# A two-layer trunk of five attention branches: branch B's V product with stationary values, the opening's loads and norms in another order, and six steps of the schedule moved

## The chip, the core and the metric

The kernel runs on one core of a Trainium2 chip. Its engines are TensorE (PE: matmuls and transposes; PEld is its weight load), VectorE (DVE), ScalarE (ACT), GpSimd (POOL) and SyncE (SP, which issues nearly all DMAs). The metric is the device time of one launch in microseconds; lower is better. Tensors are float32; operands of fast matmuls are float32r pairs, a head and the rest that the head leaves.

## The reference

```python
def hybrid_layer(x, mem, ...):                  # x 512 x 1024, mem 256 x 1024
    pr = split_projection(x @ w_in)             # q, k, v of A to E, indexer, z, g
    o_a = dsa_attention(aq, ak, av, iq, ik, pr['i_w'])   # top 128 keys by indexer
    o_b = moba_attention(bq, bk, heads(pr['b_v'], N_HEADS, HEAD_DIM))
    o_c = rms_norm(diff_attention(cq, ck, cv, lam), diff_norm) * (1.0 - lam_init)
    o_d = mla_attention(qn, qr, kn, kr, dv)
    mkv = (mem @ w_mem_kv).reshape(b, mem.shape[1], 2, N_HEADS, HEAD_DIM)
    o_e = memory_attention(heads(pr['e_q'], N_HEADS, HEAD_DIM), mkv[:, :, 0], mkv[:, :, 1])
    y = o * jax.nn.silu(pr['z'].reshape(b, t, N_BRANCH, BRANCH_W))
    u = jnp.einsum('btnc,ncd->btnd', y, w_branch)
    g = jax.nn.sigmoid(pr['g'].reshape(b, t, N_BRANCH, d))
    out = jnp.sum(g * u, axis=2) @ w_out
    return layer_norm(DN_ALPHA * x + out, ln_g, ln_b)

h = layer_norm(x, ln0_g, ln0_b)                 # then hybrid_layer, twice
```

Each branch has 4 heads of 64. B is block-sparse, but with 512 tokens and blocks of 256 every earlier block is chosen, so it is plain causal attention.

## The kernel before

**Tiling.** The 512 tokens are 4 tiles of 128; D = 1024 is 8 slabs of 128. A product of float32 accuracy is three passes (`product3`, L811 to L813): head by head, rest by head, head by rest. Weights come by DMA into raw slots; ACT rounds their head, POOL subtracts for the rest (L795): a `split` step.

**The list.** `plan()` writes one list of steps that every engine walks in order, doing its own share of each. Its backbone is `grp` steps, PE's products: chunk c, unit u (two slabs of a projection chunk, or 128 output columns of a gate chunk), part t. The chunks follow ORDER: IX (the indexer), E, A1, A0, B1, B0, gE0, gE1, gB0, gB1, C0, C1, gA0, gA1, D0, D1, DU, gC0, gC1, gD0, gD1, O0, O1. A gate chunk's unit has four parts for the gate and a fifth (t = 4) for the branch product; behind the fifth DVE multiplies the two (L1712). Attention steps are spread between two groups named in PLACES. Since an engine never passes an entry of its own list, a step that waits holds back everything behind it on that engine.

**Attention steps.** `qt` transposes queries and keys on PE (L993, L1002), `ev` and `er` copy head and rest out (ACT, then DVE; for D L1534 and L1536), `S` is the scores (L1036) with mask and maximum on DVE (L1591) and exponential on ACT, `T` transposes probabilities (L1049), `V` multiplies by the values. A unit i is head i // 4, tile i % 4; tile t has t + 1 key blocks. Branches in WIDE take `wide_steps`: V has the values' head and rest side by side as the stationary operand and moves the probabilities, also as head and rest (L1066, 4 or 8 matmuls a pair of tiles, up to 256 columns). For that DVE also computes the rest of the probabilities (`pr`, L1464) and of the values (`vr`, L1456), adds up the halves (`fa`, L1471, L1477) and multiplies later (`fin`, L1489). The other branches take the narrow V: probabilities stationary, 64 columns of values moving in plain float32 (L1083: 2, 4, 6 and 8 matmuls for the tiles of a head, 20 in all). The indexer's top 128 of each row are found by sixteen rounds of MAX8 and MATCH_REPLACE8 on DVE (`top`, `take`).

**Branch C** has two maps, hence two scores a unit; its `fin` (L1615 to L1619) takes the norm's squares. **DU** expands D's latents; its part t lies in two PSUM banks which ACT empties (L1107, `mla_keys` among them), and two pairs of banks alternate.

**The opening of layer 0.** SP loads mem, x tile 0, quarter 0 of the memory weights (mk0), the norm's gains, x1, its bias, mk1, x2, mk2, mk3, then weights, x3 among them. `mkv` multiplies the memory by mk0 to mk3 in two halves (L908, L911); `ln0` normalizes tile t (sums, root, scale, ACT's L1116, gain L1374; the bias is POOL's for tiles 0 and 1, DVE's L1379 for 2 and 3); `xj` transposes a tile (L930), ACT and DVE make it the stationary head and rest (L1445). ACT's queue writes the transposed memory to DRAM (1 MB) for layer 1. The first product of IX follows `mv`, ACT's copy of the memory values.

**The end.** Behind O1's parts DVE adds the residual (L1719) and normalizes (`l1`, `l2`), tile by tile.

## Time and profile before

| | us |
|---|---|
| three timed runs, median (lowest to highest) | 1339.69 (1339.42 to 1339.84) |
| the profiled execution, its own time | 1343.1 |
| its span in the trace | 1341.5 |
| PE busy | 1307.1 |
| DVE, POOL, ACT busy | 707.8, 663.4, 662.8 |
| mean granted clock | 0.995 |

How to read it: PE is busy in nearly the whole span, so an idle or longer stretch of PE is what time can be won from or lost to; the other engines matter where PE waits for them. Matmuls overlap in the trace, so a group's own time is from its start to the next group's start, some 0.16 us less than its span. Rows in brackets `[0.65 <-DVE ...]` give the idle time before and what ended it.

### The profile page before, as it was taken

How to read it: one execution, taken by the hardware profiler on the slowest of the kernel's cores; microseconds unless marked ns; L12 is line 12 of the kernel's file. 1: busy time of each engine (PE TensorE's matmuls, PEld its weight loads, DVE VectorE, ACT ScalarE, POOL GpSimd, SP SyncE). 2: the span in 40 equal slices, each digit the busy share in tenths (PEclk: the TensorE clock that was granted, in tenths of full speed). 3: DMA queues.
4: the chain of work that ended last, by engine and by line, in shares of the span. 5: the costliest groups of instructions: out<-in, count | busy, mean ns of one | idle time of the engine just before them, and what ended most of it. 6: DMA issues, size and time to landing. Idle time of an engine off the chain costs nothing.

```text
span 1341.5 us, 18893 instructions
## 1 busy us (share of the span) xinstructions
PE 1307.1 (97%) x6744; PEld 1108.3 (83%) x6744; DVE 707.8 (53%) x1700; ACT 662.8 (49%) x1326; POOL 663.4 (49%) x838
## 2 busy tenths in 40 slices
PE   6999999999999999999999999999999999999996
PEld 5888888888888998888887888888888889888885
DVE  4746686554347464513355577675534664454135
ACT  3555445365477475523235552554646665654232
POOL 3443453354565454467435335434445553645774
PEclk8999999999999999999999999999999999999998
DMA  7322232132332143242413223322223213323321
GB/s 278 105 79 64 83 98 79 50 94 64 87 98 59 45 120 109 59 112 77 137 42 109 79 64 92 97 60 73 83 63 103 71 52 88 101 60 92 92 91 63
DMA packets 147053, 116.47 MB, mean 87 GB/s; under 512 B 5520, under 2 KB 131856, under 8 KB 146704
## 3 DMA queue, kind: packets, MB, share of 16 engines
q1 hardware_dynamic: 146816, 114.22, 28.9%
q8 instruction: 54, 0.88, 0.3%
q10 hardware_dynamic: 144, 1.05, 0.2%
q14 instruction: 39, 0.32, 0.1%
HBM read 112.10 MB, written 3.15 MB: 86 GB/s over the span
## 4 chain that ended last, share of the span: by engine, by line
PE 80%; DVE 12%; ACT 4%; issue 2%; DMA 1%; SPq 0%; DVEq 0%; ACTq 0%
PE product L811 19%; PE product L813 18%; PE product L812 18%; PE scores L1036 3%; PE context L1083 3%; PE transposed L1049 3%; PE branch_product L811 3%; PE branch_product L812 3%; PE branch_product L813 3%; PE context L1066 2%; ACT score_operands L1107 1%; DVE index_scores L1568 1%; PE product L911 1%; DVE top_eight L1574 1%; DMA merged<-in_w_mem_kv_dram 1%
## 5 line engine op out<-in xcount | busy, mean ns | idle before, releaser
L795 POOL TENSOR_TENSOR weights_rest<-raw_weights,weights_head 128x320 fp32r<-128x320 f32 (+3 forms) x672 | 542.5, 838 | 391.4 <-ACT weights_head L1107 391.2
L811 PE MATMUL product<-weights_head,stationary_head 128*128 128x512 f32 (+3 forms) x768 | 290.7, 379 | 3.0 <-issue 2.1
L813 PE MATMUL product<-weights_head,stationary_rest 128*128 128x512 f32 (+3 forms) x768 | 284.6, 371 | 0.0
L812 PE MATMUL product<-weights_rest,stationary_head 128*128 128x512 f32 (+3 forms) x768 | 284.5, 370 | 0.0
L1107 ACT ACTIVATE weights_head<-raw_weights 128x1280 fp32r<-128x1280 f32 (+4 forms) x178 | 197.7, 1113 | 142.1 <-PE product L813 116.5
L811 PE MATMUL product<-stationary_head,weights_head 128*128 128x512 f32 x640 | 260.4, 407 | 0.0
L813 PE MATMUL product<-stationary_head,weights_rest 128*128 128x512 f32 x640 | 250.4, 391 | 0.0
L812 PE MATMUL product<-stationary_rest,weights_head 128*128 128x512 f32 x640 | 250.3, 391 | 0.0
L780 POOL TENSOR_TENSOR merged<-merged,activated 128x256 f32<-128x256 f32 x128 | 94.0, 756 | 242.5 <-DVE activated L1712 242.5
L811 PEld LDWEIGHTS product<-weights_head,stationary_head 128*128 128x128 f32 x768 | 144.7, 188 | 25.5 <-issue 3.0
L813 PEld LDWEIGHTS product<-weights_head,stationary_rest 128*128 128x128 f32 x768 | 144.5, 188 | 23.8
L812 PEld LDWEIGHTS product<-weights_rest,stationary_head 128*128 128x128 f32 x768 | 144.9, 189 | 19.8
L1241 ACT ACTIVATE probabilities<-probabilities,negated_maxima 128x256 f32<-128x256 f32 (+3 forms) x160 | 86.3, 539 | 136.3 <-DVE negated_maxima L1591 134.1
L813 PEld LDWEIGHTS product<-stationary_head,weights_rest 128*128 128x128 f32 x640 | 120.1, 188 | 26.9
L811 PEld LDWEIGHTS product<-stationary_head,weights_head 128*128 128x128 f32 x640 | 120.5, 188 | 20.3
L812 PEld LDWEIGHTS product<-stationary_rest,weights_head 128*128 128x128 f32 x640 | 120.8, 189 | 19.3
L1712 DVE SCALAR_TENSOR_TENSOR activated<-activated,branch_product 128x512 f32<-128x512 f32 x64 | 43.9, 686 | 131.6 <-PE branch_product L813 128.8
L1306 ACT ACTIVATE activated<-product 128x512 f32<-128x512 f32 x80 | 47.8, 597 | 124.3 <-PE product L813 124.1
L1591 DVE CUSTOM_DVE_ANT_0 probabilities<-scores,consts_sb 128x256 f32<-128x256 f32 (+3 forms) x136 | 60.4, 444 | 62.9 <-PE scores L1036 62.0
L1036 PE MATMUL scores<-score_operands 128*128 128x256 f32 (+7 forms) x288 | 77.3, 323 | 2.5 <-DVE negated_maxima L1591 2.4
L1036 PEld LDWEIGHTS scores<-score_operands 96*128 96x128 f32 (+1 forms) x288 | 52.1, 189 | 15.0 <-DVE negated_maxima L1591 6.8
L811 PE MATMUL branch_product<-branch_out_T_head,weights_head 128*128 128x512 f32 x160 | 64.1, 400 | 0.0
(232 smaller groups left out, 1879.1 us busy)
## 6 DMA issues: line engine op xcount, KB each, us to landing
raw_weights<-in_w_in_dram SPq DMA_DIRECT2D x104, 512.0 KB, 3.7
raw_weights<-in_w_in_dram SPq DMA_DIRECT2D x72, 256.0 KB, 2.9
raw_weights<-in_w_branch_dram SPq DMA_DIRECT2D x80, 128.0 KB, 3.7
raw_weights<-in_w_out_dram SPq DMA_DIRECT2D x16, 512.0 KB, 3.7
merged<-in_w_mem_kv_dram SPq DMA_DIRECT2D x8, 512.0 KB, 7.2
raw_weights<-in_w_in_dram SPq DMA_DIRECT2D x8, 416.0 KB, 3.1
raw_weights<-in_w_in_dram SPq DMA_DIRECT2D x8, 296.0 KB, 4.6
residual<-in_x_dram SPq DMA_DIRECT2D x4, 512.0 KB, 11.5
```

The lines of the kernel that those rows point to most:

```text
L780: ins = nc.gpsimd.tensor_tensor(m[:, part], m[:, part], TH[:, s, part], ALU.add)
L795: ins = nc.gpsimd.tensor_tensor(WL[:, sw, part], RAW[:, sr, part], WH[:, sw, part].bitcast(F32), ALU.subtract)
L811: nc.tensor.matmul(dst, sh, mh, start=start, stop=False)
L812: nc.tensor.matmul(dst, sh, ml, start=False, stop=False)
L813: return nc.tensor.matmul(dst, sl, mh, start=False, stop=stop)
L1036: last = nc.tensor.matmul(S[:, 0:w], lhs, rhs, start=i == 0, stop=i == len(passes) - 1)
L1049: last = nc.tensor.transpose(TP[:, i * P:(i + 1) * P], src[:, i * P:(i + 1) * P], ident)
L1107: return nc.scalar.activation(dst, src, ACT.Copy, scale=scale)
L1241: nc.scalar.activation(p, p, ACT.Exp, bias=NMX[:, m:m + 1], scale=-1.0, accum_out=RS[:, j % 2, 2 * t + u % 2 if b == "C" else t:(2 * t + u ...
L1306: nc.scalar.activation(TH[:, s, :], G[u % 2][:], ACT.Tanh, scale=0.5).then_inc(act_out.sem, act_out.step((c, u)))
L1591: nc.vector.tensor_tensor_reduce(probs(b, u)[:, 0:w], S[:, 0:w], bias, -SCALE[b], -TAKEN, ALU.add, ALU.min, NMX[:, u % 4:u % 4 + 1]).then_ ...
L1712: nc.vector.scalar_tensor_tensor(out=TH[:, s, :], in0=TH[:, s, :], scalar=1.0, in1=U[:], op0=ALU.add, op1=ALU.mult).then_inc(used.sem, not ...
```

## The change

Seven things, all in the list of steps or in what they touch:

1. **Opening.** mk1 is loaded directly behind mk0, then gains, bias (with a semaphore of its own), x1; mk2, mk3 come behind the first raw weights, x2 and x3 behind the second. The memory's write to DRAM is issued at `ek`. `mkv` waits for each piece of memory and weights as it comes to it. `ln0` is split into sums, scale and gain, and the start of the list is written in another order.
2. **IX.** Group (2, 2) stands ahead of (0, 3), and tile 3's `xj` stands between the two (in both layers); `ek` comes behind (0, 3). The index transposes begin at (E, 0, 3).
3. **B** is in WIDE. Its attention begins at (gE0, 1, 0) instead of (gE0, 0, 4); the rounds for tile 3 run from (gE0, 3, 0) to (gB0, 0, 1) instead of (gE0, 2, 0) to (gE1, 3, 4).
4. **C**: `fin` of heads 0 to 2 comes one step later in the list.
5. **DU**: part 2 uses the banks G2 and G3.
6. **D** attention begins at (gC0, 0, 3) instead of (gC0, 0, 2).
7. **The end**: `l2` of tile 1 comes behind group (O1, 3, 2) instead of (O1, 2, 2).

```diff
-WIDE = "AD"
+WIDE = "ABD"
@@ diff_steps
-                second.append(("fin", "C", (i - 3) // NT))
+        if i >= 7 and i % NT == 3 or i == UNITS + 2:
+            second.append(("fin", "C", (i - 4) // NT if i % NT == 3 else NH - 1))
@@ PLACES
-    ("index transposes", ("E", 0, 2), ("E", 2, 1), 0.0),
+    ("index transposes", ("E", 0, 3), ("E", 2, 1), 0.0),
-    ("B attention", ("gE0", 0, 4), ("gE1", 3, 3), 0.0),
-    ("top of tile 3", ("gE0", 2, 0), ("gE1", 3, 4), 0.0),
+    ("B attention", ("gE0", 1, 0), ("gE1", 3, 3), 0.0),
+    ("top of tile 3", ("gE0", 3, 0), ("gB0", 0, 1), 0.0),
-    ("D attention", ("gC0", 0, 2), ("gC1", 3, 3), 0.0),
+    ("D attention", ("gC0", 0, 3), ("gC1", 3, 3), 0.0),
@@ plan
-    start = [("ln0", 0), ("ln0", 1), ("ez",), ("mkv", 0), ("ln0", 2), ("xj", 0, 0), ("xj", 0, 1), splits[0], splits[1], ("ln0", 3),
-             ("mkv", 1), ("xj", 1, 0), ("xj", 1, 1), ("mv",), splits[2], ("ln0", 4)]
+    start = [("ln0", 0, part) for part in ("sums", "scale", "gain")]
+    start += [("ln0", 1, "sums"), splits[0], ("ln0", 1, "scale"), ("ln0", 1, "gain"), ("mkv", 0), ("xj", 0, 0), ("xj", 0, 1), ("ez",),
+              splits[1], ("ln0", 2, "sums"), ("ln0", 2, "scale"), ("ln0", 3, "sums"), ("ln0", 2, "gain"), ("mkv", 1), ("mv",),
+              ("xj", 1, 0), ("xj", 1, 1), ("ln0", 3, "scale"), splits[2]]
-    extra[at[(ORDER[0], 1, 1)]] += [("xj", 2, 0), ("xj", 2, 1)]
-    extra[at[(ORDER[0], 2, 1)]] += [("xj", 3, 0), ("xj", 3, 1)]
-    extra[at[(ORDER[0], 2, 2)]].append(("ek",))
+    extra[at[(ORDER[0], 1, 1)]] += [("xj", 2, 0), ("xj", 2, 1), ("ln0", 3, "gain")]
+    extra[at[(ORDER[0], 2, 2)]] += [("xj", 3, 0), ("xj", 3, 1)]
+    extra[at[(ORDER[0], 0, 3)]].append(("ek",))
-    extra[at[("O1", 2, 2)]].append(("l2", 1))
+    extra[at[("O1", 3, 2)]].append(("l2", 1))
@@ DU's banks
+            return {1: (("U", U), ("TP", TP)), 2: (("G2", G[2]), ("G3", G[3]))}.get(t, (("S", S), ("O", O)))
@@ SP's loads of the opening
             load_mk(0, 0)
+            load_mk(0, 1)
             sp.dma_start(LN_IN[:, 0:D], ln0_g.partition_broadcast(P)).then_inc(first_ln_in.sem, first_ln_in.step(("first", 0), 16))
+            sp.dma_start(LN_IN[:, D:2 * D], ln0_b.partition_broadcast(P)).then_inc(first_lb_in.sem, first_lb_in.step(("first", 1), 16))
             load_x(1)
...
+                    if L == 0 and i == 1:
+                        load_mk(0, 2)
+                        load_mk(0, 3)
                     if L == 0 and i == 2:
+                        load_x(2)
                         load_x(3)
@@ mkv on PE
+                                if L == 0:
+                                    pe.wait_ge(moved.sem, moved.at(0, ("first", kk // 2)))
                                 pe.wait_ge(mk_in[kk // 2].sem, mk_in[kk // 2].at(L, ("mk",)))
```

The lines of the changed program are some 10 to 14 higher than those of before.

**PE, the indexer's products of tile 3.** `product0` to `product3` are the banks of tiles 0 to 3, `residual` the normalized tile that L930 transposes. Before:

```order
L813 MATMUL product1<-weights_head,stationary_rest 128x296
L930 MATMUL transposed<-consts_sb,residual 128x128 [waits first_gained,rest_of_stationary]
L930 MATMUL transposed<-consts_sb,residual 128x128 x3
L930 MATMUL context<-consts_sb,residual 128x128 [waits first_gained,rest_of_stationary]
L930 MATMUL context<-consts_sb,residual 128x128 x3
L811 MATMUL product2<-weights_head,stationary_head 128x296 [waits rest_of_stationary,transposed_moved]
...
L811 MATMUL product3<-weights_head,stationary_head 128x296 [waits rest_of_stationary,transposed_moved]
```

And now (L942 is L930, L821 is L811):

```order
L823 MATMUL product1<-weights_head,stationary_rest 128x296
...
L823 MATMUL product2<-weights_head,stationary_rest 128x296
L942 MATMUL transposed<-consts_sb,residual 128x128 [waits first_gained,rest_of_stationary]
L942 MATMUL transposed<-consts_sb,residual 128x128 x3
L942 MATMUL context<-consts_sb,residual 128x128 [waits first_gained,rest_of_stationary]
L942 MATMUL context<-consts_sb,residual 128x128 x3
L821 MATMUL product3<-weights_head,stationary_head 128x296 [waits rest_of_stationary,transposed_moved]
```

Twelve matmuls of tile 2's two units lay between the transposes of tile 3 and its first product; with (1, 2) and (2, 2) now ahead of the transposes, none does.

**DVE, C's attention, around the `fin` of head 1.** L1591 is the mask and maximum of a score, L1530 the rest of a key, L1615 to L1619 the `fin`. Before:

```order
L1591 ISA probabilities,negated_maxima<-scores,consts_sb 128x384 [waits scores_done]
L1591 ISA negated_maxima 128x1
L1615 TENSOR_TENSOR vector_scratch<-diff_out 128x256 [waits scores_masked,squares_summed]
L1617 TENSOR_TENSOR values_and_gates<-values_and_gates,diff_out 128x4x64 [waits normed]
L1619 TENSOR_REDUCE diff_norm_sums<-vector_scratch 128x4 [waits vector_step]
L1530 TENSOR_TENSOR score_operands<-product3,score_operands 32x512 [waits transposed_moved]
L1591 ISA index_scores,negated_maxima<-scores,consts_sb 128x512 [waits scores_done]
L1591 ISA negated_maxima 128x1
```

And now:

```order
L1660 SCALAR_TENSOR_TENSOR probabilities<-probabilities,map_factors 128x384 [waits vector_step]
L1726 SCALAR_TENSOR_TENSOR activated<-activated,branch_product 128x512 [waits branch_product_done,activated_ready]
L1605 ISA index_scores,negated_maxima<-scores,consts_sb 128x512 [waits scores_done]
L1605 ISA negated_maxima 128x1
L1629 TENSOR_TENSOR vector_scratch<-diff_out 128x256 [waits scores_masked,squares_summed]
L1631 TENSOR_TENSOR values_and_gates<-values_and_gates,diff_out 128x4x64 [waits normed]
L1633 TENSOR_REDUCE diff_norm_sums<-vector_scratch 128x4 [waits vector_step]
L1605 ISA probabilities,negated_maxima<-scores,consts_sb 128x128 [waits scores_done]
```

The `fin` stood ahead of a key's rest and of a score of 512 keys; it now stands behind two such scores and a gate product.

**DVE, the start of D's attention.** L1494 is C's output, L1534 and L1536 the rests of D's first and second transposed queries and keys (`er`), L1712 the gate product, which waits for PE's branch product of (gC0, 0). Before:

```order
L1494 TENSOR_TENSOR branch_out_T_rest<-transposed,branch_out_T_head 128x512 [waits transposed_moved]
L1494 TENSOR_TENSOR branch_out_T_rest<-branch_product,branch_out_T_head 128x512 [waits transposed_moved]
L1534 TENSOR_TENSOR score_operands<-product2,score_operands 96x512 [waits transposed_moved]
L1536 TENSOR_TENSOR score_operands<-product3,score_operands 96x512 [waits transposed_moved]
L1712 SCALAR_TENSOR_TENSOR activated<-activated,branch_product 128x512 [waits branch_product_done,activated_ready]
L1534 TENSOR_TENSOR score_operands<-product2,score_operands 96x512 [waits transposed_moved]
```

And now:

```order
L1508 TENSOR_TENSOR branch_out_T_rest<-transposed,branch_out_T_head 128x512 [waits transposed_moved]
L1508 TENSOR_TENSOR branch_out_T_rest<-branch_product,branch_out_T_head 128x512 [waits transposed_moved]
L1726 SCALAR_TENSOR_TENSOR activated<-activated,branch_product 128x512 [waits branch_product_done,activated_ready]
L1548 TENSOR_TENSOR score_operands<-product2,score_operands 96x512 [waits transposed_moved]
L1550 TENSOR_TENSOR score_operands<-product3,score_operands 96x512 [waits transposed_moved]
L1548 TENSOR_TENSOR score_operands<-product2,score_operands 96x512 [waits transposed_moved]
```

The gate product of (gC0, 0) has come ahead of the first `er`. PE's second `qt` of D needs that `er` in both programs, since the bank is read by it.

## Rows read from the trace of the kernel before

**Rows 1.** The page: busy time by engine; shares of the last-ending chain.

```profile
PE 1307.1 (97%) x6744; PEld 1108.3 (83%) x6744; DVE 707.8 (53%) x1700; ACT 662.8 (49%) x1326; POOL 663.4 (49%) x838
...
PE 80%; DVE 12%; ACT 4%; issue 2%; DMA 1%; SPq 0%; DVEq 0%; ACTq 0%
```

**Rows 2.** The waits of PE: line waited for, us in total, times, longest.

```profile
PE branch_product L908 <- DMA merged<-in_w_mem_kv_dram: 3.8, 1, 3.8
PE scores L1036 <- DVE negated_maxima L1591: 2.4, 6, 0.6
PE product L811 <- issue: 2.1, 2, 1.1
PE transposed L963 <- DVE merged L1685: 1.7, 2, 0.9
PE product L993 <- DVE staged_features L1349: 1.4, 2, 0.7
...
PE scores L811 <- ACT mla_keys L1107: 1.3, 2, 0.6
```

**Rows 3.** Timeline of PE, 17 to 34 us: start, us, line, count, [idle <-releaser].

```profile
17.70 1.22 PE L908 MATMUL branch_product<-staged_features,merged 128*128 128x256 f32 x2 [3.83 <-DMA merged<-in_w_mem_kv_dram]
...
24.93 0.60 PE L908 MATMUL branch_product<-staged_features,merged 128*128 128x256 f32 x2
...
31.84 0.60 PE L930 MATMUL transposed<-consts_sb,residual 128*128 128x128 f32 x4
...
33.93 0.38 PE L811 MATMUL product<-weights_head,stationary_head 128*128 128x296 f32 x1 [1.06 <-issue]
```

**Rows 4.** Windows: busy time by engine, granted clock, DMA share, GB/s.

```profile
16.60:23.40 6.80, 5.70 (x13) 4.54 (x14) 4.32 (x10) 1.72 (x3) 2.95 (x5) 0.50 1.03 399
```

**Rows 5.** Timeline of PE, 39 to 50 us.

```profile
39.79 0.60 PE L930 MATMUL transposed<-consts_sb,residual 128*128 128x128 f32 x4
...
42.49 0.37 PE L811 MATMUL product<-weights_head,stationary_head 128*128 128x296 f32 x1
...
46.14 0.40 PE L811 MATMUL product<-weights_head,stationary_head 128*128 128x296 f32 x1
...
49.91 0.50 PE L811 MATMUL product<-weights_head,stationary_head 128*128 128x512 f32 x1 [0.23 <-POOL weights_rest L795]
```

**Rows 6.** Timeline of PE, 217 to 222 us: B's narrow V.

```profile
217.37 1.00 PE L1083 MATMUL context<-values_and_gates,probabilities_T 128*128 128x64 f32 x8
...
221.46 0.33 PE L1083 MATMUL context<-values_and_gates,probabilities_T 128*128 128x64 f32 x2
```

**Rows 7.** Timeline of PE, 293 to 295 us: A's wide V.

```profile
293.83 1.10 PE L1066 MATMUL context<-score_operands 128*128 128x256 f32 x8
```

**Rows 8.** Windows of B's attention and the rounds of tile 3, layer 0.

```profile
192.00:264.00 72.00, 71.30 (x398) 61.07 (x397) 46.53 (x117) 37.98 (x78) 23.70 (x29) 1.00 0.25 69
```

**Rows 9.** DVE by shape, 264 to 345 us: count, busy, mean ns, idle.

```profile
L1464 DVE TENSOR_TENSOR score_operands<-transposed,score_operands 128x512 fp32r<-128x512 f32 x4 | 2.8, 691 | 3.3 <-ACT score_operands L1107 3.1
...
L1456 DVE TENSOR_TENSOR score_operands<-values_and_gates,score_operands 128x256 fp32r<-128x256 f32 x4 | 2.6, 648 | 0.7 <-ACT score_operands L1107 0.7
```

**Rows 10.** Timeline of PE, 413 to 436 us: two scores of C.

```profile
413.99 0.50 PE L1036 MATMUL scores<-score_operands 96*128 96x512 f32 x1 [0.65 <-DVE negated_maxima L1591]
...
435.47 0.50 PE L1036 MATMUL scores<-score_operands 96*128 96x512 f32 x1 [0.24 <-DVE negated_maxima L1591]
```

**Rows 11.** Timeline of DVE, 410 to 413 us: a `fin` of C.

```profile
411.21 0.95 DVE L1617 TENSOR_TENSOR values_and_gates<-values_and_gates,diff_out 128x256 f32<-128x256 f32 x1
```

**Rows 12.** Timeline of PE, 502 to 504 us: D's second `qt`.

```profile
503.49 0.61 PE L993 MATMUL product<-consts_sb,staged_features 128*96 128x128 f32 x4 [0.26 <-DVE score_operands L1536]
```

**Rows 13.** Timeline of DVE, 505 to 508 us.

```profile
506.04 0.69 DVE L1712 SCALAR_TENSOR_TENSOR activated<-activated,branch_product 128x512 f32<-128x512 f32 x1 [2.70 <-PE branch_product L813]
...
507.25 0.68 DVE L1536 TENSOR_TENSOR score_operands<-product,score_operands 96x512 fp32r<-96x512 f32 x1
```

**Rows 14.** Timeline of DVE, 1326 to 1330 us: the end.

```profile
1327.89 1.23 DVE L1374 TENSOR_TENSOR residual<-residual,values_and_gates 128x1024 f32<-128x1024 f32 x1 [1.31 <-ACT residual L1116]
```

More of the change, by code:

```diff
@@ L258, in plan @@
         if c == "IX":
-            order = [(0, 0), (1, 0), (0, 1), (1, 1), (2, 0), (2, 1), (0, 2), (1, 2), (0, 3), (2, 2), (1, 3), (2, 3)] + [(3, t) for t in range(NT)]
+            order = [(0, 0), (1, 0), (0, 1), (1, 1), (2, 0), (2, 1), (0, 2), (1, 2), (2, 2), (0, 3), (1, 3), (2, 3)] + [(3, t) for t in range(NT)]
         elif c == "O1":
@@ L758, in _ @@
                 for step in PLAN:
-                    if step[0] == "ln0" and L == 0 and 0 < step[1] <= BIASED:
-                        offset(0, step[1] - 1, ("first", step[1] - 1), LN_IN[:, D:2 * D], gained0, normed0)
+                    if step[0] == "ln0" and L == 0 and step[2] == "gain" and step[1] < BIASED:
+                        pool.wait_ge(first_lb_in.sem, first_lb_in.at(0, ("first", 1)))
+                        offset(0, step[1], ("first", step[1]), LN_IN[:, D:2 * D], gained0, normed0)
                     if step[0] == "l2" and step[1] < BIASED:
@@ L895, in _ @@
                         if kh == 0:
-                            for name, _ in banks:
-                                claim(name)
-                            if L == 0:
-                                for j in range(4):
-                                    pe.wait_ge(moved.sem, moved.at(0, ("first", j)))
-                            else:
+                            claim("U")
+                            claim("S")
+                            if L > 0:
                                 pe.wait_ge(memt_in.sem, memt_in.at(0, ("first",)))
@@ L909, in _ @@
                                                  start=kk == 0, stop=kk == KD - 1)
+                            if kk == 0:
+                                claim("G0")
+                                claim("G1")
                             for j in range(2):
@@ L1136, in _ @@
                         copy(WH[:, w_slot(L, item), 0:n], RAW[:, raw_slot(item), 0:n]).then_inc(head.sem, head.step(step))
-                    elif kind == "ln0" and L == 0 and step[1] < NT:
+                    elif kind == "ln0" and L == 0 and step[2] == "sums":
                         t = step[1]
@@ L1387, in _ @@
                     if kind == "ln0":
-                        t = step[1]
-                        if L == 0 and t < NT:
+                        t, part = step[1:]
+                        if L > 0:
+                            continue
+                        if part == "sums":
                             dve.wait_ge(x_in[t].sem, x_in[t].at(0, ("first", t)))
```

43 lines of the change are left out of this document (20 added, 23 removed).

## The prediction

> **What bounds the kernel now.** I read the page first, then PE's waits, then the timelines at those waits. PE is busy for 1307.1 of 1341.5 us, DVE, ACT and POOL for half of it, and four fifths of the chain that ended last are PE's [rows 1]. So the time falls only where PE gets fewer or shorter matmuls, or where one of its waits goes; it rises where a wait is added. What the reader is to see among the waits [rows 2]: 3.8 us once for mk1, and then small ones that come twice, once a layer: for the maximum of a score (2.4 in all), for weights of the indexer ("issue"), for the index transposes, for B's first transposes (L993) and for DU's keys (L811 <- ACT). The change has a part for each.
>
> The sum is made against the profiled execution: 1343.1 us, span 1341.5. It is 3.4 above the median of the timed runs, 1339.69, and I carry that distance over.
>
> **1, 2. The opening.** Before, the sixth load, mk1, lands at 17.70, PE having waited 3.83 us [rows 3]; the clock granted from 16.6 to 23.4 was 0.50, that is 1.2 GHz [rows 4]; the first product of IX starts at 33.93 [rows 3]. Afterwards mk1 follows mk0 and is there when needed, so the clock should stay up. Half of `mkv` takes 6.9 us at full clock (24.93 to 31.84) [rows 3], so two halves and two `xj` (0.87 each) from about 9.7 would end at 9.7 + 2 x 6.9 + 1.7 = 25.2. PE then waits for ACT's copy of the memory values, which stands behind the root of tile 3 on ACT, and that behind DVE's sums of tile 3. The tiles' loads are not the limit: at 1.35 us a load x3 lands near 22. DVE is the later: from x1's landing (near 15) it has sums 1.5, scale 0.9, gain 1.2, rests 1.3, zeroing 1.4, sums 1.5, scale 0.9, sums 1.5 and a hop to ACT and back, in all 11.4, to 26.4. IX starts at about 27.1: 6.8 us earlier.
>
> Most of this is lost again, for DVE's list is the limit behind it. Gain and bias of tile 2 (2.5), rests of `xj` 1 (1.3), scale of tile 3 (0.5), on ACT the normalization (1.2) and `xj` 2, rests, gain and bias of tile 3 (together 5) bring tile 3's transposes to 38.45, against 39.79 before [rows 5]. From these transposes to the first product of tile 3 it took 2.70 us (39.79 to 42.49) [rows 5]: 0.87 is the transposes' own, and 1.5 of the rest was covered by the twelve matmuls that stood between; now nothing stands between, 1.8 are waited instead of 0.3. Then unit 3 waits for its weights, whose split hangs on (0, 3): 2.75 from the end of (0, 3) to 46.14 before [rows 5], less cover now, 1.1 instead of 0.4. I get the first product of E at 48.0 against 49.91 [rows 5]: **-1.9**. The wait for the index transposes, 0.84 [rows 2], shrinks by 0.6: **-2.5** for the layer. Bounds: -7.4 (6.8 and 0.6), if none of it is given back, and +0.5.
>
> Layer 1 has no such opening: the tiles are normalized long before. There the weights of IX are waited for less, since `mv` is off their path: -1.2; the two new waits cost +1.5 and +0.5, the index transposes give -0.6: **+0.2** (-1 to +2).
>
> **3. B.** Narrow V: the 8 matmuls of tile 3 have a span of 1.00, the 2 of tile 0 one of 0.33; less the 0.16 that overlap with what follows, 0.84 and 0.17 [rows 6]; with 4 and 6 between them, 2.0 a head, 8.0 a layer. Wide V: 8 matmuls take 1.10 less 0.16, 0.94 [rows 7], 4 take half: 1.4 a head, 5.65 a layer. Gain 2.35. The number of other transposes is unchanged (`zj` takes the place of those of the output). B's first transposes wait 0.7 for DVE's rotation [rows 2]; one part later the rotation is done: -0.85 with the drain. DVE gets more: rests of the probabilities 2.8 for the 512 columns [rows 9], 7 to 8 for all widths, rests of values 2.6 [rows 9], halves and products some 3, less 3.5 of the narrow form, some 10 in all. The stretch has 46.5 busy of 72 [rows 8]; with 56, less what the rounds' later end takes out, it is 54 or 55. PE needs 70 there, so DVE still ends in time, but the list is dense and I add 0.4 for small waits. **-2.8 a layer, -5.6.** Bounds: -3.2 and +4 a layer (see the rivals).
>
> **4. C.** `fin` begins at 410.8 in front of a score's maximum, its middle operation alone takes 0.95 [rows 11], and PE waits 0.65 for that maximum at 413.99 [rows 10], 0.8 with the drained pipe. The next `fin` does the same at 435.47, 0.24 idle [rows 10], 0.4 in all; the two are part of the six waits in 2.4 [rows 2]. Behind the scores it holds up only the reciprocals of the sums. **-1.0 a layer, -2.0.** Bounds: 0 and -1.2.
>
> **5. DU.** Part 2 waits for ACT to empty the first pair of banks, 0.6 a layer [rows 2], 0.8 with the drain. G2 and G3 have no user between. **-1.6.** Bounds: 0 and -1.6.
>
> **6. D.** Here the change adds a wait. Before, `er` of the first transposes stood ahead of the gate product and PE's second `qt` waited 0.26 for it [rows 12], 0.4 with the drain. Now DVE's gate product of (gC0, 0), which can't begin before PE has finished the branch product, stands ahead of both rests, and PE's second `qt`, directly behind that branch product in PE's list, waits for the rests. In the old trace the gate product begins 0.27 after PE's last matmul, and from its start (506.04) to the end of the second rest behind it (507.25 + 0.68) 1.9 us pass [rows 13]; with the signal 2.3. Queued behind the waiting `qt` is all of PE's list. 2.3 - 0.43 = **+1.87 a layer, +3.75.** Bounds: 0, if the rests could pass, and +4.5.
>
> **7. The end.** DVE idles 1.31 for ACT in front of tile 2's gain [rows 14] and now has tile 1's norm there or later; the last residual comes 0.85 earlier. **-0.85.** Bounds: 0 and -1.3.
>
> **Sum:** -2.5 + 0.2 - 5.6 - 2.0 - 1.6 + 3.75 - 0.85 = -8.6. Profiled execution 1334.5; median of the timed runs **1331.1**.
>
> **The rivals.** (a) The gain of the opening is kept whole. For: PE's IX starts 6.8 earlier, and a list spread over 15 us has slack that I may have double-counted. Against: x3's gain and bias are serial behind the sums. -4.3 more: 1327.
>
> (b) The clock falls again. Between 24 and 42 us PE would have gaps of 2.0, 1.5, 1.6 and 1.8 us. Before, PE's last matmul ahead of the wait ended at 13.9 (17.70 - 3.83), and 2.7 us later the granted clock was at half, until 23.4 [rows 3, 4]; a pair of `mkv` matmuls took 1.22 there and 0.60 at full clock [rows 3]. Seven us at half speed cost 3.5: 1334.5. Short gaps have not lowered it elsewhere in this trace. The Trainium skill (TensorE: Matmul & The Clock Gate, "A second HAM failure mode: psum-queue depth-cycling") tells of a kernel whose many small idle times between groups of matmuls made the clock go back and forth; by that rule (b) would happen, by the rows it happened only behind one long wait.
>
> (c) **DVE becomes the bound in B's stretch.** The rests of the probabilities stand in the same list as the sixteen rounds for tile 3, PE's V waits for them, and DVE may run slower beside a busy POOL. For: where DVE had most to do in C, PE waited 0.65 [rows 10], and an operation of `fin` on 256 columns took 0.95 [rows 11], half as long again as the 0.65 of another of that width [rows 9]. Against: 54 of 72. It decides from the point where DVE's work grows by a third over 54 (72). At 1.38 times, DVE needs 74.5, 4.3 us more than PE, and the change gives nothing (8.6 lost over two layers): 1339.7. At 1.42 times it is 6 or more a layer, the time 1343: slower than before. The Trainium skill (GPSIMD Engine Reference, "1. Specifications") says that GpSimd shares its SBUF interface with VectorE and that instructions with two SBUF inputs contend there. By that rule the values' rests (two SBUF inputs) would suffer, and they average 648 ns for 256 columns [rows 9]; the probabilities' rests read one input from PSUM, and stand at 691 for 512 with POOL busy half the time [rows 8, 9], so most of the added work should not grow.
>
> (d) The opening gives nothing (+2.5), C and DU keep a third of their waits (+1.2), and D's wait is at its upper bound (+1.5): 5.2 more, 1336.3. For it speaks that each of the small waits has another event close behind it; against it, that the three are independent.
>
> **How the numbers follow.** My forecast (1328.5 to 1334) 0.48; (a) 0.13; (b) 0.15; (d) 0.09; (c) within 0.2% of before 0.10, slower by more 0.05. 0.2%, 2.7 us, is about what a measurement of this kernel can tell from no change. Faster by more than that: 0.48 + 0.13 + 0.15 + 0.09 = 0.85, within 0.10, slower 0.05. The range reaches from rival (a) less 1.5 us of the bounds to the end of (d), 1325.5 to 1337; outside lie (c), 0.15, and 0.04 below.
>
> **What would show it.** E's first product at about 48, IX's at 27, granted clock 1.0 from 10 us on; PE idle 1.8 ahead of tile 3's first IX product in each layer; no waits of PE for the rotation (L1349), for `mla_keys`, or for the two maxima behind `fin`; 48 more wide matmuls a layer and 80 fewer narrow ones; PE idle over 2 us on D's second `qt`, ended by DVE. The prediction is wrong if PE waits in B's attention for rests of the probabilities, if IX starts later than 29, or if D's `qt` waits under 1 us.

## The result, and the profile after

| | before | changed |
|---|---|---|
| timed runs, median (us) | 1339.76 | 1349.55 |
| lowest to highest | 1339.42 to 1342.49 | 1348.18 to 1350.44 |
| ratio, 95% interval | | 1.0068 (1.0056 to 1.008) |
| span of the profiled execution | 1341.5 | 1347.7 |
| PE busy | 1307.1 | 1301.9 |
| DVE busy | 707.8 | 730.6 |

The change makes the kernel 9.8 us slower. It was forecast 8.6 us faster, with slower at 0.05. PE does have less to do (1307.1 to 1301.9, as the shorter V of B foretold), so the loss is waits: in B's attention PE now idles for an operation of DVE ahead of most of the V products, and D's start costs more than it was priced at. The page of the changed kernel, busy time and shares of the chain, against [rows 1]:

```profile
PE 1301.9 (97%) x6680; PEld 1101.5 (82%) x6680; DVE 730.6 (54%) x1744; ACT 670.1 (50%) x1342; POOL 664.2 (49%) x838
...
PE 84%; DVE 8%; ACT 5%; issue 2%; DMA 1%; POOL 0%; SPq 0%; DVEq 0%; ACTq 0%
```

The waits of PE in the changed kernel (line waited for, us in total, times, longest), against [rows 2]. L1078 is the wide V (L1066 of before), L1470 the rest of B's values, L1478 the rest of its probabilities, L1005 D's transposes, L821 a product's first pass:

```profile
PE context L1078 <- DVE score_operands L1470: 8.7, 6, 1.7
...
PE context L1078 <- DVE score_operands L1478: 4.7, 6, 1.2
PE product L821 <- DVE stationary_rest L1459: 4.6, 3, 1.7
PE product L1005 <- DVE score_operands L1550: 4.3, 2, 2.1
PE product L821 <- POOL weights_rest L805: 2.8, 3, 0.9
...
PE product L821 <- issue: 1.1, 1, 1.1
...
PE scores L1048 <- DVE negated_maxima L1605: 0.6, 2, 0.3
```

What the reader is to see: the wait for mk1 is gone, and so are the one for B's rotation and the one for DU's keys; those for score maxima fell from 2.4 to 0.6. The lines leave out PE's wait for its first load, which is in both kernels (5.5 and 5.3). New are 8.7 + 4.7 us of the wide V for DVE, 4.6 for the stationary rest in the indexer, and 4.3 for D's second `qt`.

The two programs have the same 4776 product matmuls, in the same order but for a few of IX, so the start of the n-th in one trace less that in the other says where time went:

| stretch (products) | forecast, a layer | layer 0 | layer 1 |
|---|---|---|---|
| opening to B (to 576; 2304 to 2928) | -2.5; +0.2 | -3.5 | +0.3 |
| B's attention and the rounds (576 to 864; 2928 to 3216) | -2.8 | +4.6 | +4.7 |
| C (1344 to 1440; 3696 to 3840) | -1.0 | -1.4 | -1.4 |
| DU (1680 to 1728; 4032 to 4112) | -0.8 | -1.1 | -1.1 |
| D (1728 to 1968; 4112 to 4320) | +1.9 | +3.8 | +2.4 |
| the end (behind 4752) | -0.85 | | -1.0 |

The columns of layer 0 and of layer 1 add up to +6.2, the difference of the two spans. The forecast held to about half a microsecond everywhere except in B, 15 us off in both layers together, and in D, 2.4 off; the opening is a case of its own. Of the 3.6 us between 6.2 and the 9.8 of the timed runs, 2.2 are in the trace of before, as x4 shows below; 1.4 stay open.

**The opening** went by the numbers of the prediction, compared with the trace that it was made from. Timeline of PE in the changed kernel (start, us, line, count, [idle <-releaser]), against [rows 3] and [rows 5]:

```profile
26.71 0.37 PE L821 MATMUL product<-weights_head,stationary_head 128*128 128x296 f32 x1 [1.11 <-issue]
...
37.66 0.60 PE L942 MATMUL transposed<-consts_sb,residual 128*128 128x128 f32 x4
...
40.43 0.37 PE L821 MATMUL product<-weights_head,stationary_head 128*128 128x296 f32 x1 [1.74 <-DVE stationary_rest L1459]
...
44.07 0.40 PE L821 MATMUL product<-weights_head,stationary_head 128*128 128x296 f32 x1 [0.94 <-POOL weights_rest L805]
...
47.44 0.40 PE L821 MATMUL product<-weights_head,stationary_head 128*128 128x512 f32 x1
```

IX starts at 26.71 (forecast 27.1), tile 3's transposes at 37.66 (38.45), PE then idles 1.74 for their rest (1.8) and 0.94 for the weights of unit 3 (1.1), and E starts at 47.44 (48.0).

**B.** Timeline of PE in the changed kernel, the first four idle times in B's attention, against [rows 7]:

```profile
213.29 1.20 PE L1078 MATMUL context<-score_operands 128*128 128x256 f32 x8 [0.96 <-DVE score_operands L1478]
...
221.48 0.70 PE L1078 MATMUL context<-score_operands 128*128 128x256 f32 x4 [1.71 <-DVE score_operands L1470]
...
228.72 1.21 PE L1078 MATMUL context<-score_operands 128*128 128x256 f32 x8 [1.15 <-DVE score_operands L1478]
...
236.60 0.70 PE L1078 MATMUL context<-score_operands 128*128 128x256 f32 x4 [1.40 <-DVE score_operands L1470]
```

And DVE's list ahead of the second of them:

```profile
218.32 0.68 DVE L1485 TENSOR_TENSOR probabilities_T<-context,probabilities_T 64x512 f32<-64x512 f32 x1 [1.40 <-ACT probabilities_T L1119]
218.93 0.68 DVE L1588 MAX8 top_eight<-index_scores 128x8 f32<-128x512 f32 x1
219.53 0.66 DVE L1723 SCALAR_TENSOR_TENSOR merged<-activated,branch_product 128x512 f32<-128x512 f32 x1
220.12 0.41 DVE L1478 TENSOR_TENSOR score_operands<-transposed,score_operands 128x256 fp32r<-128x256 f32 x1
220.45 0.93 DVE L1470 TENSOR_TENSOR score_operands<-values_and_gates,score_operands 128x256 fp32r<-128x256 f32 x1
```

DVE first idles 1.40 for ACT's copy. L1485 then adds up the halves of the head before (`fa`), then come a round of tile 3 (MAX8), a gate product, the probabilities' rest and the values' rest; they run back to back from 218.3 to 221.4, and PE's V of the new head needs the last. The windows view of the stretch, against [rows 8]:

```profile
192.00:264.00 72.00, 65.35 (x342) 53.76 (x341) 52.96 (x126) 38.44 (x81) 23.00 (x27) 1.00 0.21 59
```

DVE is busy for 53.0 of 72 us: the load is what was forecast (54 or 55), and yet PE is idle for over 6 us. Where the text says that PE loses time ahead of V, the wait is counted with its drained pipe: from the start of the last matmul ahead of it to the start of the next, less the 0.23 us of a matmul of 512 columns. So counted, PE loses 7.6 us ahead of V in layer 0 and 7.7 in layer 1.

### The profile page after: what moved, and what is told of

It reads as the page before. It is cut to its first block, busy times and chain, and to the rows that moved or that the text cites. A ratio compares the mean times of both kernels' runs of the same rounds, so it can differ in the third digit from the quotient of the medians.

```text
span 1347.7 us, 18838 instructions
## 1 busy us (share of the span) xinstructions
PE 1301.9 (97%) x6680; PEld 1101.5 (82%) x6680; DVE 730.6 (54%) x1744; ACT 670.1 (50%) x1342; POOL 664.2 (49%) x838
## 4 chain that ended last, share of the span: by engine, by line
PE 84%; DVE 8%; ACT 5%; issue 2%; DMA 1%; POOL 0%; SPq 0%; DVEq 0%; ACTq 0%
PE product L821 21%; PE product L823 20%; PE product L822 20%; PE scores L1048 3%; PE branch_product L821 3%; PE transposed L1061 3%; PE branch_product L823 3%; PE context L1078 3%; PE branch_product L822 3%; PE context L1095 2%; ACT score_operands L1119 2%; DVE top_eight L1588 1%; DVE index_scores L1571 1%; DVE index_scores L1582 1%; ACT weights_head L1119 1%
## 5 line engine op out<-in xcount | busy, mean ns | idle before, releaser
L821 PE MATMUL product<-weights_head,stationary_head 128*128 128x512 f32 (+3 forms) x768 | 290.4, 378 | 8.8 <-DVE stationary_rest L1459 4.6
L821 PE MATMUL product<-stationary_head,weights_head 128*128 128x512 f32 x640 | 259.4, 405 | 0.0
L821 PEld LDWEIGHTS product<-weights_head,stationary_head 128*128 128x128 f32 x768 | 144.7, 188 | 31.6 <-issue 7.1
L821 PEld LDWEIGHTS product<-stationary_head,weights_head 128*128 128x128 f32 x640 | 120.7, 189 | 20.6
L821 PE MATMUL branch_product<-branch_out_T_head,weights_head 128*128 128x512 f32 x160 | 64.9, 406 | 0.0
L822 PE MATMUL branch_product<-branch_out_T_rest,weights_head 128*128 128x512 f32 x160 | 62.6, 391 | 0.0
```

The costliest lines, as they stand in the source:

```text
L821: nc.tensor.matmul(dst, sh, mh, start=start, stop=False)
L822: nc.tensor.matmul(dst, sh, ml, start=False, stop=False)
```

## The experiments

The runs were timed beside the kernel before; its medians there were 1340.79 (x1 to x4), 1341.09 (x5 to x8) and 1340.63 (x9, x10), where it was 1339.76 beside the changed kernel. So a distance between two runs of different groups is good to about 1 us; the distances by stretch, from the traces, are not touched by this.

### x1: B narrow

```diff
-WIDE = "ABD"
+WIDE = "AD"
```

> The changed kernel with B taken out of WIDE again, everything else as changed (B attention still from the first part of gE0's unit 1, the rounds of tile 3 still late). Theory R (DVE's list is too full for wide V beside the sixteen rounds of tile 3): PE's waits on DVE in B's attention (14.5 us in both layers in the changed kernel) go, the 2.35 us a layer of shorter V go too: per layer -7.5 + 2.35 = -5.2, so about 1339 us against 1349.6. Rival P (the later places of B attention or of the rounds are at fault, not the wide V): the waits stay, time about 1354.

Measured: 1339.44 us (1338.29 to 1340.87), ratio 0.9989 (0.998 to 0.9999). The theory's number; rival P's 1354 is out. All of PE's waits on L1470 and L1478 in B are gone, and the stretch costs 5.4 us a layer less than wide. So the later places did no harm; the wide V did. The same trace keeps B's gain from the rotation that is now done in time: 0.93 a layer at that place, of which 0.8 is left at the end of the stretch.

### x2: the rounds of tile 3 on 16 columns

```diff
-                        dst = SC[:, SC_W[t]:SC_W[t] + (t + 1) * P]
+                        dst = SC[:, SC_W[t]:SC_W[t] + (16 if t == NT - 1 else (t + 1) * P)]
```

> The changed kernel, but the sixteen rounds of tile 3 look at 16 columns of the 512 instead of all: that leaves the choice of A's keys for tile 3 out, and takes some 20 us of DVE work out of B's attention in each layer, no instruction and no wait. Theory R: PE's waits on DVE in B's attention fall from 7.2 us a layer to under 1: -12 to -14 us, about 1336. Rival L (the wide V of B waits for its rests because of DVE's own waits for ACT's copies, whatever else DVE has to do): at least half of the waits stay, 1343 or more.

Measured: 1342.45 us (1340.90 to 1343.07), 7.1 less than the changed kernel, where 12 to 14 were expected. The run leaves out the choice of A's keys for tile 3 and stands here for its time alone. PE's waits in B:

```profile
PE context L1078 <- DVE score_operands L1470: 2.9, 5, 0.7
...
PE context L1078 <- DVE score_operands L1478: 1.4, 2, 0.7
```

They fell from 13.4 to 4.3 us, but they did not vanish: in layer 0, 3.2 of 7.6 us lost ahead of V remain with hardly any rounds. The rounds are more than half of it, and the rest has a cause of its own. Neither text on this run holds: theory R expected waits under 1 us a layer, rival L at least half of them. Not all of the 4.4 us that went need be the rounds' own work: the four values' rests of layer 0 also took 1.7 us here against 2.9 in the changed kernel (see rival (c) below). Even without the rounds' load, wide B is no faster than narrow B with them (x1).

### x3: the rounds earlier

```diff
-    ("top of tile 3", ("gE0", 3, 0), ("gB0", 0, 1), 0.0),
+    ("top of tile 3", ("B0", 3, 0), ("gE0", 3, 4), 0.0),
```

> The changed kernel with the rounds of tile 3 moved from (gE0,3,0)..(gB0,0,1) to (B0,3,0)..(gE0,3,4), so that half of them lie ahead of B's attention. Nothing is left out. Theory R: B's heads 1 to 3 run free, the first may wait 1 us: -5 to -6.5 us a layer, 1337 to 1340. Rival L: under 2 us a layer, above 1345.

Measured: 1362.90 us (1362.11 to 1362.97), 13.4 slower than the changed kernel. Theory R is missed by over 20 us; the time is above the 1345 of rival L, but not by its reason, since the waits of V did fall. PE's waits:

```profile
PE product L1005 <- DVE staged_features L1360: 7.3, 2, 3.6
PE scores L1048 <- DVE negated_maxima L1605: 5.8, 6, 1.6
...
PE context L1078 <- DVE score_operands L1470: 4.2, 5, 1.4
...
PE context L1078 <- DVE score_operands L1478: 2.2, 4, 0.7
```

B's V waits less (6.4 for 13.4), but the rounds now stand ahead of B's rotation, for which PE's first `qt` waits 3.6 us in each layer, and ahead of the maxima of B's first scores (5.8, of which 0.6 are C's as in the changed kernel). Behind both waits of 3.6 the granted clock fell to half as well. The room in front of B's attention is not free: the same work was merely put where PE is nearer to waiting for DVE.

### x5: the rests of B's operands behind the unit's own

```diff
-            first.append(("er", b, 1 + i // 4))
+            (second if b == "B" else first).append(("er", b, 1 + i // 4))
```

> The changed kernel, with the rests of B's third and fourth transposed operands (er of heads 2 and 3) moved on DVE from in front of a unit's probability rest (pr) to behind it and behind the unit's score; nothing else. Theory E (DVE's own waits inside its list: er waits for ACT's copies, 1.0 and 0.5 us, and pr, for which PE's V waits, is queued behind it): PE's two waits a layer of V for a probability rest of four key blocks (L1478: 4.7 us in 6) fall to about 1 in all, those for the value rests (L1470: 8.7) stay: -3 to -4 us against 1349.6. Rival T (throughput only: DVE has as much to do as before): unchanged within 1 us.

Measured: 1347.77 us (1347.33 to 1350.46), ratio to before 1.0052 (1.0037 to 1.0067), 1.8 less than the changed kernel and 0.4 below its lowest run. The traced execution is the slowest of the four, 1350.46. PE's waits:

```profile
PE context L1078 <- DVE score_operands L1470: 6.8, 6, 1.4
...
PE context L1078 <- DVE score_operands L1478: 2.5, 4, 1.1
PE transposed L1061 <- DVE score_operands L1478: 2.4, 4, 0.8
```

The waits of V for L1478 fell from 4.7 to 2.5, but 2.4 came back as waits of PE's transposes (L1061) for the same L1478: the next unit's transposes need the PSUM bank `TP`, and in the wide form the bank is free only when DVE has taken the rest out of it. By the products' starts B's stretch gained 0.3 us in layer 0 and 0.4 in layer 1, where theory E expected 3 to 4 in all. The other 1.1 of the 1.8 are not explained by it; the granted clock can make them, since its mean was 0.998 in the three faster runs of x5, and in one of four of the changed kernel. So moving DVE's waits about inside its list is worth little. That there are two places, V and the next transposes, at which PE hangs on each rest is what the prediction's "PE's V waits for them" left out; in the changed kernel itself PE idled at V alone.

### x8 and x10: A's attention squeezed, wide and narrow

```diff
-    ("A attention", ("gB0", 0, 2), ("C0", 1, 2), 0.0),
+    ("A attention", ("gB0", 0, 2), ("gB1", 3, 0), 0.0),
```

and for x10 also `WIDE = "BD"`.

> The changed kernel with A's attention spread over 36 parts, from (gB0,0,2) to (gB1,3,0), instead of 42, about as dense as B's 34; A's attention is wide too and has no rounds beside it. Theory S (a wide attention this dense has too little PE work between a unit's transposes and its V, whatever DVE has to do): PE waits of 0.7 to 0.9 us at V appear in A, two to four a layer, time +3 to +6. Rival (it takes DVE's other load too): under 0.5 us a layer.

> The run with A's attention squeezed to 36 parts, but A out of WIDE too (B and D stay wide). Theory S with its link (the waits come by the wide form's chain: PE's V and PE's next transposes wait for DVE's rest of the probabilities, where the narrow form waits for ACT's copy alone): no PE wait above 0.3 us at V in A; A's stretch loses the 4.2 us a layer that squeezing cost and pays 2.35 for the narrow V: about 2 us a layer less than with A wide, 1351 to 1352. Rival (any attention this dense starves PE): waits for ACT or DVE in the same places, 1355 or more.

The 42 and 36 parts of the two texts are 45 and 34 by the places: A's attention has 45 in the changed kernel and 34 in these two, as many as B's. Measured: x8 1355.56 us, one run, 6.0 above the changed kernel. A's attention has no rounds, and DVE had half its time free; still PE now lost 3.9 us in it in layer 0, in three waits of 0.4 to 1.5 and some small ones, where it had lost 0.3. By the products' starts A's stretch costs 3.3 us more in layer 0 and 3.5 in layer 1; 1.5 come back because the clock did not fall behind D's wait. The rival's 0.5 us a layer is out. x10: 1357.60, one run. Windows of A's stretch, x8 and then x10:

```profile
270.00:345.00 75.00, 71.98 (x371) 59.36 (x370) 36.50 (x87) 39.85 (x84) 36.63 (x48) 1.00 0.26 71
```

```profile
270.00:345.00 75.00, 75.00 (x410) 64.24 (x409) 25.86 (x66) 37.88 (x77) 38.94 (x51) 1.00 0.25 71
```

With A narrow, PE has no idle time in the 75 us, and no wait above 0.3 us at a V. That half of the expectation held. The time of the run did not come down, though: it lies in the rival's range (1355 or more), while the waits that the rival needs are not there. By the products' starts A's stretch takes 1.6 us less than in x8 in layer 0 and 1.5 less in layer 1, with the longer matmuls paid, where about 2 was expected; but the granted clock fell to half three times where in x8 it did not, once behind a wait of B's V (1.1 us lost) and behind D's wait in both layers (1.65 each), and the opening took 0.7 longer. So the theory's link is shown by the waits and by the stretch, not by the run's time.

The chain at a change of head, in x8, where no round can be blamed. DVE, and then PE:

```profile
321.74 0.68 DVE L1485 TENSOR_TENSOR vector_scratch<-context,vector_scratch 64x512 f32<-64x512 f32 x1 [1.39 <-ACT vector_scratch L1119]
322.85 0.69 DVE L1726 SCALAR_TENSOR_TENSOR activated<-activated,branch_product 128x512 f32<-128x512 f32 x1 [0.42 <-PE branch_product L823]
323.45 0.42 DVE L1478 TENSOR_TENSOR score_operands<-transposed,score_operands 128x256 fp32r<-128x256 f32 x1
323.79 0.83 DVE L1470 TENSOR_TENSOR score_operands<-values_and_gates,score_operands 128x256 fp32r<-128x256 f32 x1
```

```profile
324.72 0.70 PE L1078 MATMUL context<-score_operands 128*128 128x256 f32 x4 [1.53 <-DVE score_operands L1470]
```

`fa` has to wait for ACT's copy (1.39 idle ahead of it), then for the gate product's matmuls, then come the two rests, 0.42 and 0.83; PE has used up its work by then and idles 1.53 (322.85 to 324.62 are DVE's gate product and rests back to back).

### x6: D's attention back

```diff
-    ("D attention", ("gC0", 0, 3), ("gC1", 3, 3), 0.0),
+    ("D attention", ("gC0", 0, 2), ("gC1", 3, 3), 0.0),
```

> The changed kernel with D's attention back at (gC0,0,2). Theory D: the wait of D's second qt (2.30 us in each layer) falls to the 0.43 of before, -3.7 us, about 1345.9. Rival: D's later steps sit one part differently and take some of it back; the two waits of 0.69 and 0.39 later in D's attention stay or grow, gain under 2.5 us.

Measured: 1343.89 us (1343.35 to 1345.07), 5.7 less than the changed kernel; 3.7 was expected. The wait fell as expected:

```profile
PE product L1005 <- DVE score_operands L1550: 0.6, 2, 0.3
```

The rest has two parts. In layer 1, where the clock stayed up, D's stretch is still 2.4 us shorter than in the changed kernel, 0.5 more than the 1.9 of the wait: further on, at 548.1 in layer 0 and 1209.8 in layer 1, the changed kernel's transposes in D wait 0.53 for a rest of DVE's, which is most of these 0.5 (such a wait was 0.15 before). The other part is the clock, 1.5 us in layer 0. In the changed kernel the wait was 2.14 us of idle time, as forecast (2.3 with the drained pipe), against [rows 12]:

```profile
505.32 1.06 PE L1005 MATMUL product<-consts_sb,staged_features 128*96 128x128 f32 x4 [2.14 <-DVE score_operands L1550]
```

but behind it, in layer 0, the granted clock was at half, 1.2 GHz, and in layer 1, behind the same wait, it was not:

```profile
505.00:506.80 1.80, 1.48 (x7) 1.45 (x8) 0.17 (x1) 0.38 (x1) 1.80 (x3) 0.55 0.03 9
506.80:508.40 1.60, 1.60 (x7) 1.30 (x6) 1.19 (x2) 1.11 (x3) 1.60 (x3) 0.50 0.00 0
1166.00:1169.00 3.00, 0.86 (x7) 0.51 (x6) 1.88 (x3) 1.27 (x1) 1.74 (x3) 1.00 0.39 114
1168.40:1173.00 4.60, 4.47 (x24) 3.87 (x25) 1.65 (x3) 1.38 (x3) 3.79 (x5) 1.00 0.01 4
```

The matmuls of 512 columns behind the wait in layer 0 started 0.43 us apart instead of 0.23; the D stretch cost 3.8 us in layer 0 and 2.4 in layer 1. With D's place as changed there are seven traces, fourteen such waits, and the clock fell behind eight: both of x2, x5 and x10, one of x1 and of the changed kernel, none of x3 and x8. In x6 and x9, without the wait, it did not fall there.

### x4 and x7: the trace of before, and the opening alone

x4 is the kernel before once more. x7 is the kernel before with parts 1 and 2 of the change only.

> The kernel before, unchanged, for one more trace of it. Its profiled execution took 1343.1 us, 3.4 above the median of the timed ones. Theory C (the granted clock falls in the opening in some executions and not in others, by where the 3.8 us wait for mk1 falls): a trace with a time near 1339.7 shows the second half of mkv at full clock and the first product of IX some 3 us earlier than 33.93, everything behind alike. Rival: the 3.4 us lie elsewhere, and the first product of IX is again at 33.9.

> The kernel before with the opening, the order of IX and the place of the index transposes changed, and nothing else (B narrow and in its old place, rounds, C's fin, DU's banks, D and the end as before). Against a trace of before whose clock stayed up in the opening (first product of IX at 31.65, of E at 47.6) the forecast by terms is: E's first product -0.2, index transposes -0.9, layer 1 +0.3: -0.8 us, the same within the noise. Rival: the opening is worth the -3.5 us that the first pair of traces shows, ratio 0.9975.

Measured: x4 1340.88, one run, span 1339.2. PE and the granted clock in its opening, against [rows 3] and [rows 4]:

```profile
9.83 1.19 PE L908 MATMUL branch_product<-staged_features,merged 128*128 128x256 f32 x2 [1.07 <-DMA merged<-in_w_mem_kv_dram]
...
13.37 0.64 PE L908 MATMUL branch_product<-staged_features,merged 128*128 128x256 f32 x2
...
18.21 0.70 PE L908 MATMUL branch_product<-staged_features,merged 128*128 128x256 f32 x2 [2.90 <-DMA merged<-in_w_mem_kv_dram]
...
31.65 0.37 PE L811 MATMUL product<-weights_head,stationary_head 128*128 128x296 f32 x1 [1.06 <-POOL weights_rest L795]
```

```profile
16.60:23.40 6.80, 5.19 (x28) 4.65 (x29) 4.10 (x9) 1.63 (x3) 2.87 (x6) 1.00 1.04 399
```

The wait for mk1 is there (2.90), but the clock stayed at 1.00 behind it, the pairs of `mkv` matmuls took half as long, and IX starts at 31.65 instead of 33.93. All products behind stand 2.2 to 2.3 us earlier than in the first trace, and the span is 2.2 shorter. From the landing of mk1 to IX it takes 13.4 us here and 16.2 before, so the fall itself cost 2.8, near the theory's 3; mk1 landed 0.5 later here. Of the 3.4 us by which that execution lay above the median, 2.2 are this.

The wait is shorter because PE was slow ahead of it. A pair of `mkv` matmuls still takes 1.19 at 9.83 and 0.64 from 13.37 on: here PE came up to full speed only near 13.4, where in the first trace the pair that starts at 10.18 already took 0.67, and so its work ahead of the wait ended at 15.3 instead of 13.9. In the ten traces with the changed opening the first record of the full clock lies between 7.8 and 15.0 us; IX starts between 26.6 and 28.05, latest in the trace with the latest record (x10), though not in step with it everywhere.

x7: 1340.32 us (1340.02 to 1341.00), ratio 0.9994 (0.9985 to 1.0004). Against x4, its IX starts 4.9 earlier and E 0.1 earlier, the index transposes give 1.0, layer 1 takes 0.4 back: -0.7. The rival's ratio of 0.9975 is out. The opening is worth under 1 us in a median run. The -3.5 of the table above compares with an execution whose clock had fallen.

### x9: what the runs point to

```diff
-WIDE = "ABD"
+WIDE = "AD"
-    ("D attention", ("gC0", 0, 3), ("gC1", 3, 3), 0.0),
+    ("D attention", ("gC0", 0, 2), ("gC1", 3, 3), 0.0),
-    extra[at[(ORDER[0], 2, 2)]] += [("xj", 3, 0), ("xj", 3, 1)]
+    extra[at[(ORDER[0], 1, 2)]] += [("xj", 3, 0), ("xj", 3, 1)]
```

> The changed kernel with B narrow, D's attention back at (gC0,0,2), and tile 3's transposes (xj) one group earlier, behind (1,2) instead of (2,2); opening, C's fin, DU's banks and the end as changed. By the ledger of the traces: 1339.4 (B narrow) less the 5.7 that D's place was worth, of which up to 1.6 may have been a fall of the clock behind the wait, less 0.8 in layer 1: 1333 to 1334.5, ratio to before about 0.995. Rival: the gains of C, DU and the end (2.8, 1.8 and 0.9) overlap with what D gives back, 1337.

Measured: 1331.55 us (1330.84 to 1331.65), ratio 0.9928 (0.9914 to 0.9941): 9.1 us faster than before and 18 faster than the changed kernel; that is 1.5 us below the expected 1333 to 1334.5. Its busy times and two of PE's waits:

```profile
PE 1302.2 (98%) x6744; PEld 1107.3 (83%) x6744; DVE 706.6 (53%) x1700; ACT 663.1 (50%) x1326; POOL 663.0 (50%) x838
```

```profile
PE product L821 <- DVE stationary_rest L1459: 3.0, 3, 1.2
PE product L821 <- POOL weights_rest L805: 2.8, 3, 0.9
```

The transposes of tile 3 one group earlier gave 0.8 in each layer (from IX's start to B's stretch 155.0 us in layer 0, against 155.8 in the changed kernel). That was expected of layer 1 only; tile 3 was ready in time in layer 0 too. D's place gave 6.2 by the traces, with a fall of the clock in it, against the 5.7 that was counted on. With these numbers the sum comes to about 1331.6. The waits of V and of D's `qt` are at the level of before.

## Why the prediction was wrong, point by point

**Opening: right in its times.** 26.7, 37.7, 1.7, 0.9, 47.4 were forecast as 27.1, 38.45, 1.8, 1.1, 48.0. That the gain at the start is given back because DVE's list is the limit was the right mechanism. Rival (a) is out. Wrong was what it was compared with: the profiled execution of before stood 2.2 us behind x4 because of the clock, and I carried its 3.4 us above the median as a constant. A gain worked out partly from that fall can't be had in the runs that don't have it. The fall was also priced too high: seven us at half speed were to cost 3.5, but PE sat idle for the first 1.1 of them, and it cost 2.8. The error of the sum from the wrong comparison is 1.6. Rival (d) was right in this one of its three parts (the opening gives next to nothing), and wrong in C and DU, which gave more than forecast; its sum also has 1.5 for D at the upper bound, where the bounds above give 4.5 - 3.75 = 0.75.

**B: the step that failed** is "PE needs 70 there, so DVE still ends in time, but the list is dense and I add 0.4 for small waits". It was also what the prediction itself named as its sign of being wrong. The 0.4 measured 7.6. The matmul term was right: PE lost 7.6 us a layer in waits ahead of V, yet B's stretch is only 5.4 longer than with B narrow (x1), so the shorter V gives 2.2 a layer for the 2.35 forecast. The load was right too (53.0 measured, 54 or 55 worked out). Yet a sum of DVE's work over 72 us says nothing of a chain that returns to PE at every unit. In the wide form PE's V and its next transposes wait for an operation of DVE that stands behind whatever else is in the list, and behind DVE's own waits for ACT and PE. Of the 7.6 us in layer 0, 4.4 go with the rounds' load and 3.2 are left to the chain by itself (x2). x8 and x10 show the latter without any rounds: a wide attention squeezed to B's density waits, a narrow one doesn't. The trace of before had told of it: A's wide attention runs free, but over 45 parts, where B has 34.

**Rival (c)** named the right place, waiter and sign, and had 0.15 in all, 0.05 for slower. Its price and its deciding point were wrong, since both were worked out by throughput: it asked for 72 us of DVE work, and 53 were enough. Contention with POOL has a smaller part: the probabilities' rests took 0.28 to 0.69 by their width, as before. The values' rest took 0.93 in the changed kernel, with POOL at work from 220.24 on, and 0.41 in x2, begun at 219.61 ahead of POOL's start at 219.92. That is what the Trainium skill's sentence on two-input instructions says (GPSIMD Engine Reference, "1. Specifications"), and the traces agree, with 0.5 us of a wait of 1.7. Over the four values' rests of layer 0 it is 2.9 us against 1.7 in x2, so up to 1.2 of the 7.6; no run varies POOL's work alone, and the share is not measured by itself.

**C and DU: right, a little small.** -1.4 and -1.1 a layer for -1.0 and -0.8, both beyond the bounds that were set (-1.2, and -1.6 for both layers of DU, which gave -2.2).

**D: right mechanism and wait, two effects missed.** 2.30 forecast and 2.30 measured. Left out was the clock behind it, 1.5 to 1.7 us in the layers in which it falls, and 0.5 a layer from the later steps of D, which also come one part later (2.35 in the layers without a fall, for 1.87). The two layers together cost 6.2, above the bound of 4.5. Rival (b) was right in kind and wrong in place: it had the clock falling in the opening's gaps, where it never did in ten traces: the longest gap there was 1.74. It fell behind D's wait of 2.14, and in x3 behind one of 3.65. The Trainium skill's story of many small gaps (TensorE: Matmul & The Clock Gate, "A second HAM failure mode: psum-queue depth-cycling") isn't what the traces show: the stretch with the most gaps, B's with up to 1.75 us each, lowered it in one trace of seven, a single wait of 2.14 in more than half of the cases.

**The end:** -1.0 for -0.85.

With B at +4.65 a layer instead of -2.8 (+14.9), D with the clock (+2.4), the opening at the -0.7 of x7 instead of -2.3 (+1.6), and C, DU and the end (-1.7), the sum of -8.6 turns into +8.6; +9.8 was measured, and either kernel's runs spread over more than 2 us. That x9, without B's wide V and D's place, comes out at 1331.55 where 1331.1 was forecast for the changed kernel is chance: its terms are others.

## What to carry to other kernels

Before a product is given an operand that another engine must prepare at every step, count the chain from one step's result to the next step's start, with what stands in that engine's list in between, and compare it with the work that the bound engine has between the two; the engine's busy share over the stretch doesn't answer that. The same form that is free where the steps lie far apart costs more than it saves where they are dense. And take two traces of the kernel before: one of them may contain an event, here a fall of the clock in the opening, that part of the gain is then worked out from.

## What the runs showed of the hardware

TensorE's granted clock fell to 1.2 GHz behind some waits and not behind others of the same length: behind 8 of 14 waits of 2.14 us (in the changed kernel from 505.2 to 508.6), behind both of 3.65 (x3) and that of 3.83 (before), but not behind one of 2.90 (x4). Of the waits between 1.3 and 1.75 us, some forty-five in all traces, one had it (1.74, in x10). Each fall behind D's wait cost 1.5 to 1.7 us on top of the wait, the one in the opening of before 2.8. So a wait near or above two microseconds should be priced with a chance of that much more, and executions of one kernel can be 2 us apart by it. The start differs too: the first pair of `mkv` matmuls at full speed came at 10.2 in one execution of the kernel before and at 13.4 in the other (x4).

Two readings of DVE belong beside it. A subtraction of 128x256 with both inputs in SBUF (L1470) took 0.41 us when POOL began 0.3 us behind it (x2) and 0.93 with POOL at work throughout (the changed kernel). The one of the same size that reads one input from PSUM (L1478) took 0.41 and 0.42 with POOL starting in the midst of it (the changed kernel, x8).
